# First norm of a hybrid encoder block on one Trainium2 core: gain multiplied as rows land, reciprocal root applied by a diagonal product, six idle products

## The chip, the cores and the metric

The kernel runs on one core of a Trainium2 chip (trn2). A core has TensorE (PE, with its weight loads PEld), VectorE (DVE), ScalarE (ACT), GpSimd (POOL) and SyncE (SP, which only issues DMAs here), 128-partition memories SBUF and PSUM (8 banks of 512 f32 columns), and 16 DMA engines. The metric is the device time of one execution in microseconds (us).

## The reference, cut to what matters

The block works on x with 512 rows (frames) of 1024 values. The change lies in the first norm and what feeds the first projection:

```python
def rms_norm(x, g):
    xf = x.astype(jnp.float32)
    y = xf * lax.rsqrt(jnp.mean(xf * xf, axis=-1, keepdims=True) + EPS)
    return (y * g.astype(jnp.float32)).astype(x.dtype)
...
def mixer(h, w_in, ...):
    proj = h @ w_in                       # 1024 x 4136
...
    for l in range(DEPTH):                # DEPTH = 1
        h = rms_norm(x, g_mix[l])
        x = x + mixer(h, w_in[l], ...)    # conv branch, indexer with top-k, sparse attention, gates, w_out
        h = rms_norm(x, g_ffn[l])
        x = x + hier_moe(h, ...)          # routed experts, 2 of 32 for each row
    return rms_norm(x, g_final)
```

## The kernel before, in words

The program is written out by hand for each engine, with semaphores between them: `pe.wait_ge(S["h_ready"], b + 1)` makes TensorE wait until the semaphore h_ready has counted to b + 1. An engine runs its instructions in the order in which they are written, so that order is the order of the work. Nothing is scheduled by a planner.

The 512 rows lie in four blocks of 128 (b = 0 to 3, TB = 4). SyncE issues their four loads first (ld_x), ScalarE issues the load of g_mix (ld_gmix), then SyncE the small part of w_in and the first two tiles of w_in, 256 columns each.

First norm, for each block of rows:

- ScalarE squares the 1024 columns and sums them into ss (L1163), semaphore ss_done.
- VectorE makes mean square plus EPS of it (`mean_square`, L1419), semaphore var_ready.
- GpSimd raises it to the power -0.5 (L539), semaphore rstd_ready. This is the "root" of a block, rs[:, 0, b].
- VectorE scales the block with root and gain in one instruction (L1438), semaphore h_ready. The result, hrow, lies in the tile that the trace calls region.
- TensorE transposes it in eight 128x128 pieces into two PSUM banks (L693), four pieces to a bank; xt_mm counts banks, n = 2b + kh. Banks 4 to 7 are used in turn, so bank n + 4 waits for h_lo of n (hlo_ready).
- ScalarE rounds a bank to fp32r (h_hi, L1172, hhi_ready), and VectorE takes the rest, bank minus h_hi (h_lo, L1430, `h_low`, hlo_ready).

When all eight h_lo are there, TensorE starts on the projection: units 0 to 32, each with 8 steps of k, and 3 products in each step (L708: hi x hi, hi x lo, lo x hi). The weights are split in the same way: ScalarE makes part 0 (L1117, w_hi), GpSimd part 1 (L561, w_lo). Unit u + 2 is split once unit u's last product is done (unit_mm). Unit 0 has 40 columns of weights, the others 128. ScalarE's splits of units 0 and 1 stand between its h_hi 3 and h_hi 4.

Behind the projection come indexer and top-k, attention, the convolution branch, the output product, the second norm with the router, and a loop over tiles of expert rows for which SyncE streams the experts' weights.

bm is a tile of 4 x 512 columns. Its part 0 is set to zero by GpSimd at the start, its part 2 is free until the top-k. ones_b is a 128x128 bf16 tile of ones, ident the f32 identity; both are ready with consts_ready 1.

Of the kernel before, what the change touches and what calls it, by code (L numbers as in the profile page):

```python
# [19 lines left out]
BF16 = mybir.dt.bfloat16  # L20
# [3 lines left out]
ALU = mybir.AluOpType  # L24
# [3 lines left out]
P = 128  # L28
BANK = 512
# [37 lines left out]
def build(nc, x, g_mix, w_in, conv_w, conv_b, conv_ln_g, conv_ln_b, w_conv_out, w_attn_out, w_out,  # L67
          rel_bias, g_ffn, w_gr, b_gr, w_er, b_er, w_e_gate, w_e_up, w_e_down, g_final, out):
    _, T, D = x.shape
    TB = T // P  # L70
    KD = D // P
# [28 lines left out]
    with ExitStack() as ctx:  # L100
# [25 lines left out]
        hrow = r1[:, 0:4096].rearrange("p (b n) -> p b n", b=TB)  # L126
# [44 lines left out]
        score, work = bm[:, 2, :], bm[:, 3, :]  # L171
        ring = bm
# [120 lines left out]
        names = """consts_ready ss_done var_ready rstd_ready h_ready cv_mm cv_ev xt_mm hhi_ready hlo_ready  # L293
# [385 lines left out]
        def _(pe):  # L679
# [3 lines left out]
            def transpose_rows(rows, ready, mm_sem, ev_sem, banks, after=None):  # L683

                for b in range(TB):
                    pe.wait_ge(ready, b + 1)
                    view = rows[:, b, :].rearrange("p (q k) -> p k q", k=KD)
                    for kh in range(2):
                        n = 2 * b + kh
                        if n >= len(banks):  # L690
                            pe.wait_ge(ev_sem, n - len(banks) + 1)
                        for kk in range(4):
                            last = tr(bank[banks[n % len(banks)]][:, kk * P:(kk + 1) * P], view[:, 4 * kh + kk, :],  # L693
                                      ident[:])
                        last.then_inc(mm_sem, 1)
                    if after and b:
                        after(b - 1)
                if after:
                    after(TB - 1)

            transpose_rows(hrow, S["h_ready"], S["xt_mm"], S["hlo_ready"], (4, 5, 6, 7))
# [704 lines left out]
        def _(dve):  # L1406
# [25 lines left out]

            mean_square(0, 0)
            for b in range(TB):
                if b + 1 < TB:
                    mean_square(0, b + 1)
                dve.wait_ge(S["rstd_ready"], b + 1)
                v.scalar_tensor_tensor(hrow[:, b, :], xr[:, b, :], rs[:, 0, b:b + 1], gmix, ALU.mult, ALU.mult)\  # L1438
                    .then_inc(S["h_ready"], 1)
                if b >= 2:  # L1440
                    h_low(2 * b - 4)
                    h_low(2 * b - 3)
            for n in range(2 * TB - 4, 2 * TB):
                h_low(n)
# [444 lines left out]
```

## Time and profile before

| | |
|---|---|
| time, median of 3 runs | 660.34 us (658.94 to 660.87) |
| the profiled execution's own time | 660.56 us |
| its span, from the first instruction to the last | 658.5 us |
| mean granted clock of TensorE | 0.96 |
| TensorE busy | 585.3 us (89% of the span) |
| VectorE busy | 344.7 us (52%) |
| ScalarE busy | 256.3 us (39%) |
| GpSimd busy | 294.9 us (45%) |

The span is that of the profiled execution, and its own time stands 2 us above it. Busy shares are means over a program whose stages have different limits; what a change in the first 20 us is worth is to be read there. The granted clock is a share of TensorE's full 2.4 GHz.

### The profile page before, as it was taken

Reading aid. Unit: us, or ns where it says so; the run is one execution under the profiler, and the core shown is the slowest. Engines: PE = TensorE matmul, PEld = TensorE weight load, DVE = VectorE, ACT = ScalarE, POOL = GpSimd, SP = SyncE. Lnnn points to the kernel's source line nnn. Section 1 sums busy time; section 2 is a strip of 40 time slices with the busy share of each in tenths; the row PEclk is TensorE's granted clock in tenths of the full one; section 3 lists DMA queues with packets and bytes.
Section 4 is the critical chain, followed back from the end, with each engine's and each line's share of the span. In section 5 each row is a group of like instructions: output and inputs, shape, how many; then the busy total and the mean of one; then the engine's idle time right before and its main releaser. Section 6 shows DMA issues by size and latency. Waiting matters only on the chain.

```text
span 658.5 us, 12493 instructions
## 1 busy us (share of the span) xinstructions
PE 585.3 (89%) x4383; PEld 381.0 (58%) x4388; DVE 344.7 (52%) x855; ACT 256.3 (39%) x444; POOL 294.9 (45%) x466
## 2 busy tenths in 40 slices
PE   3899999999999999999999976985898899888973
PEld 3577788877666676877888632432344444444431
DVE  4428999999979996269222683110112111211156
ACT  6345333244755675454313103331243233334212
POOL 5344344469996321445550016453255445444421
PEclk9899999999999999899999697997899999999977
DMA  9032732622222024032259999999998999999853
GB/s 297 23 111 65 226 94 67 137 64 65 64 65 65 0 75 181 1 128 73 87 191 356 378 397 352 408 407 408 409 401 325 410 410 407 409 400 398 342 230 127
DMA packets 64609, 149.09 MB, mean 226 GB/s; under 512 B 14372, under 2 KB 30756, under 8 KB 64574
## 3 DMA queue, kind: packets, MB, share of 16 engines
q1 hardware_dynamic: 59150, 139.90, 57.4%
q0 software_dynamic: 5280, 8.22, 3.4%
q10 hardware_dynamic: 144, 0.52, 0.3%
q8 instruction: 20, 0.33, 0.2%
q14 instruction: 15, 0.12, 0.0%
HBM read 145.11 MB, written 12.60 MB: 240 GB/s over the span
## 4 chain that ended last, share of the span: by engine, by line
PE 56%; DVE 20%; DMA 9%; SPq 6%; issue 4%; ACT 3%; POOL 1%; DVEq 0%; POOLq 0%; ACTq 0%
PE bank L708 28%; PE bank L1026 9%; PE bank L1043 6%; DVE bm L1481 5%; SPq L433 4%; DVE m L1480 4%; DMA region<-in_w_e_down 3%; DMA conv_buf<-in_w_e_down 3%; DVE conv_buf L1472 3%; PE bank L786 2%; PE bank L989 2%; DMA region<-expert_rows 2%; PE bank L819 2%; SPq L443 2%; PE bank L936 1%
## 5 line engine op out<-in xcount | busy, mean ns | idle before, releaser
L708 PE MATMUL bank<-h_hi,w_part 128*128 128x512 f32 (+1 forms) x528 | 174.3, 400 | 1.7 <-DVE h_lo L1430 1.7
L561 POOL TENSOR_TENSOR w_part<-region,w_part 128x1024 fp32r<-128x1024 f32 (+1 forms) x52 | 109.8, 2112 | 146.5 <-ACT w_part L1117 146.5
L708 PEld LDWEIGHTS bank<-h_hi,w_part 128*128 128x128 f32 (+1 forms) x528 | 98.3, 186 | 29.1 <-issue 6.1
L708 PE MATMUL bank<-h_lo,w_part 128*128 128x512 f32 (+1 forms) x264 | 103.5, 392 | 0.0
L1807 DVE TENSOR_TENSOR mask_b<-mask_b,bank 128x128 f32<-128x128 f32 x30 | 8.6, 287 | 176.0 <-ACT mask_b L1380 101.4
L1026 PE MATMUL bank<-region,kT 128*32 128x256 f32 x1408 | 83.9, 391 | 8.8 <-DMA region<-in_w_e_up 5.8
L1117 ACT ACTIVATE w_part<-region 128x1024 fp32r<-128x1024 f32 (+1 forms) x52 | 48.0, 925 | 106.1 <-PE bank L708 105.9
L611 POOL TENSOR_TENSOR carrier<-mhalf 128x1 f32<-128x1 f32 x183 | 32.8, 197 | 114.8 <-ACT qT L1387 97.5
L1515 DVE SCALAR_TENSOR_TENSOR bank<-glu,cv,bank 128x256 f32<-128x256 f32 x196 | 78.6, 476 | 0.0
L1026 PEld LDWEIGHTS bank<-region,kT 128*32 128x32 f32 x1408 | 47.4, 113 | 51.5 <-issue 19.3
L1043 PE MATMUL bank<-region,mask_b 128*32 128x512 f32 x352 | 44.5, 624 | 12.0 <-DVE mask_b L1810 8.9
L708 PEld LDWEIGHTS bank<-h_lo,w_part 128*128 128x128 f32 (+1 forms) x264 | 49.3, 187 | 9.9 <-issue 0.5
L1387 ACT ACTIVATE qT<-bank 128x512 f32 x28 | 16.7, 597 | 84.7 <-PE bank L1043 84.7
L626 POOL DMA_INDIRECT bm<-h_rows,gi x34 | 36.5, 1073 | 5.0 <-issue 0.2
L669 POOL DMA_INDIRECT expert_rows<-qT,si x30 | 30.7, 1023 | 13.5 <-issue 13.3
L1380 ACT ACT_TABLE_LOAD x28 | 35.9, 1283 | 0.5
L1380 ACT ACTIVATE mask_b<-bank 128x128 f32<-128x128 f32 x30 | 8.3, 277 | 62.0 <-PE bank L1026 60.3
L1026 PE MATMUL bank<-gates,kT 128*32 128x256 f32 x512 | 29.4, 380 | 2.2 <-DMA gates<-in_w_e_up 1.2
L989 PE MATMUL bank<-ident,v_rows 128*128 128x128 f32 x124 | 23.5, 313 | 6.5 <-DVE v_rows L1802 5.7
L989 PEld LDWEIGHTS bank<-ident,v_rows 128*128 128x128 f32 x124 | 17.4, 209 | 20.0 <-issue 13.9
L1043 PEld LDWEIGHTS bank<-region,mask_b 128*32 128x32 f32 x352 | 9.8, 112 | 29.8 <-issue 28.4
L1026 PEld LDWEIGHTS bank<-gates,kT 128*32 128x32 f32 x512 | 16.9, 110 | 17.6 <-issue 7.3
(289 smaller groups left out, 926.2 us busy)
## 6 DMA issues: line engine op xcount, KB each, us to landing
region<-in_w_e_down SPq DMA_DIRECT2D x22, 1024.0 KB
region<-in_w_e_gate SPq DMA_DIRECT2D x44, 512.0 KB
region<-in_w_e_up SPq DMA_DIRECT2D x44, 512.0 KB
region<-in_w_in SPq DMA_DIRECT2D x16, 1024.0 KB, 6.1
conv_buf<-in_w_e_down SPq DMA_DIRECT2D x10, 1024.0 KB
gates<-in_w_e_gate SPq DMA_DIRECT2D x20, 512.0 KB
gates<-in_w_e_up SPq DMA_DIRECT2D x20, 512.0 KB
region<-in_w_out SPq DMA_DIRECT2D x2, 2048.0 KB, 8.1
```

The lines of the kernel that those rows point to most:

```text
L561: g.tensor_tensor(unit_part(u, 1), unit_raw(u), unit_part(u, 0).bitcast(F32), ALU.subtract)\
L611: ins = g.tensor_tensor(carrier[:, n:n + 1], mhalf[:], mhalf[:], ALU.add)
L626: g.indirect_dma_start(out=ring[:, u, :], out_offset=None, in_=h2_halves, in_offset=bass.IndirectOffsetOnAxis(ap=gi1[:, u:u + 1], axis=0), ...
L669: g.indirect_dma_start(out=y_halves, out_offset=bass.IndirectOffsetOnAxis(ap=si1[:, q:q + 1], axis=0), in_=ys[:, q, :], in_offset=None, bo ...
L708: last = mm(out_, a_parts[p], b_parts[q], start=start and x_ == 0, stop=stop and x_ == 2)
L989: last = tr(bank[6 + k // 2][:, k % 2 * P:(k % 2 + 1) * P], view[:, k, :], ident[:])
L1026: last = mm(bank[0][32 * c:32 * c + 32, 0:FF], xTs[:, k, at_:at_ + 32], w_gu[slot][:, e, :, half, k, j * P:(j + 1) * P], start=(half == 0 ...
L1043: last = mm(bank[2][32 * c:32 * c + 32, :], hidT[:, at_:at_ + 32], w_dn[slot][:, e, j, n * BANK:(n + 1) * BANK], start=(j == 0), stop=(j = ...
L1117: a(unit_part(u, 0), unit_raw(u), ACT.Copy).then_inc(S["w_hi"], 1)
L1380: a(sil, bank[0][:, 0:P], ACT.Silu).then_inc(S["silu_g"], 1)
L1481: link(v.match_replace(work[:, 0:n], m8[:], src[:, 0:n], NEG))
L1515: ins = v.scalar_tensor_tensor(out_, shifted, cv[:, c, j:j + 1], so_far, ALU.mult, ALU.add)
```

## The change

The gain is multiplied into a block as soon as it has landed, without the root (`gain_rows`). VectorE then makes a 128x128 diagonal with the block's roots (`rstd_diag`, into bm's part 2), and TensorE, in place of transposing with the identity, multiplies the block's pieces with that diagonal, which transposes and scales in one. Behind the products of blocks 1, 2 and 3 stand one, one and four bf16 products of 512 columns (ones_b by the zeros in bm) whose result in bank 2 nobody reads. The helper `transpose_rows`, whose `after` nobody used, is gone.

```diff
@@ -169,6 +169,7 @@
         score, work = bm[:, 2, :], bm[:, 3, :]
+        rdiag = bm[:, 2, :].rearrange("p (b n) -> p b n", b=TB)
...
@@ -680,25 +681,21 @@
             pe.wait_ge(S["consts_ready"], 1)
-            def transpose_rows(rows, ready, mm_sem, ev_sem, banks, after=None):
-
-                for b in range(TB):
-                    pe.wait_ge(ready, b + 1)
-                    view = rows[:, b, :].rearrange("p (q k) -> p k q", k=KD)
-                    for kh in range(2):
-                        n = 2 * b + kh
-                        if n >= len(banks):
-                            pe.wait_ge(ev_sem, n - len(banks) + 1)
-                        for kk in range(4):
-                            last = tr(bank[banks[n % len(banks)]][:, kk * P:(kk + 1) * P], view[:, 4 * kh + kk, :],
-                                      ident[:])
-                        last.then_inc(mm_sem, 1)
...
-            transpose_rows(hrow, S["h_ready"], S["xt_mm"], S["hlo_ready"], (4, 5, 6, 7))
+            idle_rows = bm[:, 0, :].bitcast(BF16)[:, 0:BANK]
+            for b in range(TB):
+                pe.wait_ge(S["h_ready"], b + 1)
+                pe.wait_ge(S["rdiag_ready"], b + 1)
+                view = hrow[:, b, :].rearrange("p (q k) -> p k q", k=KD)
+                for kh in range(2):
+                    n = 2 * b + kh
+                    if n >= 4:
+                        pe.wait_ge(S["hlo_ready"], n - 3)
+                    for kk in range(4):
+                        last = mm(bank[4 + n % 4][:, kk * P:(kk + 1) * P], view[:, 4 * kh + kk, :], rdiag[:, b, :],
+                                  start=True, stop=True)
+                    last.then_inc(S["xt_mm"], 1)
+                for _ in range((0, 1, 1, 4)[b]):
+                    mm(bank[2][:], ones_b[:], idle_rows, start=True, stop=True)
             pe.wait_ge(S["hlo_ready"], 2 * TB)
...
@@ -1430,17 +1427,33 @@
+            def gain_rows(b):
+
+                dve.wait_ge(ld_x[b], 16)
+                v.tensor_tensor(hrow[:, b, :], xr[:, b, :], gmix, ALU.mult).then_inc(S["h_ready"], 1)
+
+            def rstd_diag(b):
+
+                dve.wait_ge(S["consts_ready"], 1)
+                dve.wait_ge(S["rstd_ready"], b + 1)
+                v.tensor_scalar(rdiag[:, b, :], ident[:], rs[:, 0, b:b + 1], None, ALU.mult)\
+                    .then_inc(S["rdiag_ready"], 1)
+
+            gain_rows(0)
             mean_square(0, 0)
-            for b in range(TB):
-                if b + 1 < TB:
-                    mean_square(0, b + 1)
-                dve.wait_ge(S["rstd_ready"], b + 1)
-                v.scalar_tensor_tensor(hrow[:, b, :], xr[:, b, :], rs[:, 0, b:b + 1], gmix, ALU.mult, ALU.mult)\
-                    .then_inc(S["h_ready"], 1)
-                if b >= 2:
-                    h_low(2 * b - 4)
-                    h_low(2 * b - 3)
-            for n in range(2 * TB - 4, 2 * TB):
+            gain_rows(1)
+            rstd_diag(0)
+            mean_square(0, 1)
+            gain_rows(2)
+            rstd_diag(1)
+            mean_square(0, 2)
+            gain_rows(3)
+            rstd_diag(2)
+            mean_square(0, 3)
+            h_low(0)
+            h_low(1)
+            rstd_diag(3)
+            for n in range(2, 2 * TB):
                 h_low(n)
```

VectorE's queue from its first instruction on, before. The names in brackets are the semaphores waited for; ss is the mean square, region the scaled rows:

```order
L1419 TENSOR_SCALAR ss<-ss 128x1 [waits ss_done,ld_gmix]
L1419 TENSOR_SCALAR ss<-ss 128x1 [waits ss_done]
L1438 SCALAR_TENSOR_TENSOR region<-x_rows,rs,gates 128x1024 [waits rstd_ready]
L1419 TENSOR_SCALAR ss<-ss 128x1 [waits ss_done]
L1438 SCALAR_TENSOR_TENSOR region<-x_rows,rs,gates 128x1024 [waits rstd_ready]
L1419 TENSOR_SCALAR ss<-ss 128x1 [waits ss_done]
L1438 SCALAR_TENSOR_TENSOR region<-x_rows,rs,gates 128x1024 [waits rstd_ready]
L1430 TENSOR_TENSOR h_lo<-bank,h_hi 128x4x128 [waits hhi_ready] x2
L1438 SCALAR_TENSOR_TENSOR region<-x_rows,rs,gates 128x1024 [waits rstd_ready]
L1430 TENSOR_TENSOR h_lo<-bank,h_hi 128x4x128 [waits hhi_ready] x6
```

The same place in the change, from the second block's multiply on (ahead of it stand the first block's multiply, which waits for ld_x0 and ld_gmix, and its mean square; bm<-ident,rs is the diagonal):

```order
L1433 TENSOR_TENSOR region<-x_rows,gates 128x1024 [waits ld_x1]
L1439 TENSOR_SCALAR bm<-ident,rs 128x128 [waits rstd_ready,consts_ready]
L1416 TENSOR_SCALAR ss<-ss 128x1 [waits ss_done]
L1433 TENSOR_TENSOR region<-x_rows,gates 128x1024 [waits ld_x2]
L1439 TENSOR_SCALAR bm<-ident,rs 128x128 [waits rstd_ready,consts_ready]
L1416 TENSOR_SCALAR ss<-ss 128x1 [waits ss_done]
L1433 TENSOR_TENSOR region<-x_rows,gates 128x1024 [waits ld_x3]
L1439 TENSOR_SCALAR bm<-ident,rs 128x128 [waits rstd_ready,consts_ready]
L1416 TENSOR_SCALAR ss<-ss 128x1 [waits ss_done]
L1427 TENSOR_TENSOR h_lo<-bank,h_hi 128x4x128 [waits hhi_ready] x2
L1439 TENSOR_SCALAR bm<-ident,rs 128x128 [waits rstd_ready,consts_ready]
L1427 TENSOR_TENSOR h_lo<-bank,h_hi 128x4x128 [waits hhi_ready] x6
```

The 1024-column operations no longer wait for the root and all stand ahead of the first h_lo; the wait for the root has moved to four 128-column operations, the first three of which stand ahead of the next mean square.

TensorE's queue from the third block of rows to the first projection products, before:

```order
L693 MATMUL bank<-ident,region 128x128 [waits hlo_ready,h_ready]
L693 MATMUL bank<-ident,region 128x128 x3
L693 MATMUL bank<-ident,region 128x128 [waits hlo_ready]
L693 MATMUL bank<-ident,region 128x128 x3
L708 MATMUL bank<-h_hi,w_part 40x512 [waits w_lo,hlo_ready]
L708 MATMUL bank<-h_lo,w_part 40x512
```

The same place in the change, from the product behind the second block on (bm<- is the diagonal in L694, the zeros in L698):

```order
L698 MATMUL bank<-bm,ones_b 128x512
L694 MATMUL bank<-bm,region 128x128 [waits hlo_ready,rdiag_ready,h_ready]
L694 MATMUL bank<-bm,region 128x128 x3
L694 MATMUL bank<-bm,region 128x128 [waits hlo_ready]
L694 MATMUL bank<-bm,region 128x128 x3
L698 MATMUL bank<-bm,ones_b 128x512 x4
L705 MATMUL bank<-h_hi,w_part 40x512 [waits w_lo,hlo_ready]
L705 MATMUL bank<-h_lo,w_part 40x512
```

The products stand where the transposes stood, with one more semaphore to wait for, and the four idle products fill the place between the last block and the projection.

## Rows read from the trace of the kernel before

**Rows 1.** The page's part 4, the chain that ended last, by line.
```profile
PE bank L708 28%; PE bank L1026 9%; PE bank L1043 6%; DVE bm L1481 5%; SPq L433 4%; DVE m L1480 4%; DMA region<-in_w_e_down 3%; DMA conv_buf<-in_w_e_down 3%; DVE conv_buf L1472 3%; PE bank L786 2%; PE bank L989 2%; DMA region<-expert_rows 2%; PE bank L819 2%; SPq L443 2%; PE bank L936 1%
```

**Rows 2.** Chain of waits, 0 to 60 us: start us, us, what.
```profile
18.45 0.69 DVE h_lo L1430
...
19.19 23.54 PE bank L708 x96
```

**Rows 3.** Time line, GpSimd, then VectorE: start us, us, instruction [idle before <-releaser].
```profile
7.75 0.56 POOL L539 TENSOR_TENSOR rs<-ss,mhalf 128x1 f32<-128x1 f32 x1 [3.89 <-DVE ss L1419]
...
9.05 1.52 POOL L539 TENSOR_TENSOR rs<-ss,mhalf 128x1 f32<-128x1 f32 x1 [0.74 <-DVE ss L1419]
...
10.55 0.54 POOL L539 TENSOR_TENSOR rs<-ss,mhalf 128x1 f32<-128x1 f32 x1
...
12.04 1.52 POOL L539 TENSOR_TENSOR rs<-ss,mhalf 128x1 f32<-128x1 f32 x1 [0.95 <-DVE ss L1419]
...
8.89 1.28 DVE L1438 SCALAR_TENSOR_TENSOR region<-x_rows,rs,gates 128x1024 f32<-128x1024 f32 x1
...
10.61 1.28 DVE L1438 SCALAR_TENSOR_TENSOR region<-x_rows,rs,gates 128x1024 f32<-128x1024 f32 x1 [0.35 <-POOL rs L539]
...
11.87 1.27 DVE L1438 SCALAR_TENSOR_TENSOR region<-x_rows,rs,gates 128x1024 f32<-128x1024 f32 x1
...
15.46 3.67 DVE L1430 TENSOR_TENSOR h_lo<-bank,h_hi 128x512 fp32r<-128x512 f32 x6
```

**Rows 4.** Stretches: length, PE, PEld, DVE, ACT, POOL busy (xcount), granted clock, DMA, GB/s.
```profile
17.50:18.98 1.48, 0.01 (x1) 0.00 (x0) 1.48 (x3) 0.64 (x2) 1.48 (x1) 1.00 0.06 25
18.99:22.39 3.40, 3.20 (x8) 1.49 (x9) 2.50 (x32) 0.00 (x0) 0.22 (x1) 0.50 0.01 1
22.40:25.80 3.40, 3.40 (x16) 1.63 (x15) 0.04 (x1) 0.00 (x0) 0.00 (x0) 1.00 0.00 0
```

**Rows 5.** Time line, ScalarE, squares, first h_hi, first large split.
```profile
6.18 1.06 ACT L1163 ACTIVATE gates<-x_rows 128x1024 f32<-128x1024 f32 x1 [3.65 <-DMA x_rows<-in_x]
...
7.63 1.06 ACT L1163 ACTIVATE gates<-x_rows 128x1024 f32<-128x1024 f32 x1 [0.31 <-DMA x_rows<-in_x]
...
11.51 0.60 ACT L1172 ACTIVATE h_hi<-bank 128x512 fp32r<-128x512 f32 x1
...
14.85 1.05 ACT L1117 ACTIVATE w_part<-region 128x1024 fp32r<-128x1024 f32 x1
```

**Rows 6.** DMA issues, 0 to 40 us: KB, us from issue to landing.
```profile
gates<-in_g_mix ACTq DMA_DIRECT2D x1, 512.0 KB, 5.5
```

**Rows 7.** Line L1602, an existing diagonal: ns min/median/max, first and last start.
```profile
L1602 DVE TENSOR_SCALAR bm<-ident,rs x4: 278/279/289, 269.3 to 269.9; 128x128 f32<-128x128 f32 x4
```

**Rows 8.** Time line, TensorE: transposes; plain f32 products; bf16 products.
```profile
10.31 5.46 PE L693 MATMUL bank<-ident,region 128*128 128x128 f32 x24 [10.31 <-DVE region L1438]
...
16.29 1.22 PE L693 MATMUL bank<-ident,region 128*128 128x128 f32 x8 [0.52 <-DVE h_lo L1430]
...
255.29 3.67 PE L848 MATMUL bank<-conv_buf,ones 128*128 128x512 f32 x8 [1.29 <-issue]
...
367.22 1.90 PE L936 MATMUL bank<-wr,bm 128*128 128x36 f32 x8
...
384.77 3.19 PE L965 MATMUL bank<-mask_b,ones_b 128*128 128x512 bf16 x14
```

**Rows 9.** Time line, GpSimd, part 1 of unit 2's weights.
```profile
27.64 2.39 POOL L561 TENSOR_TENSOR w_part<-region,w_part 128x1024 fp32r<-128x1024 f32 x1 [8.44 <-ACT w_part L1117]
```

**Rows 10.** Stretches, columns as in rows 4; the clock falls behind the last three.
```profile
388.00:394.00 6.00, 4.18 (x96) 2.76 (x96) 3.97 (x23) 0.00 (x0) 2.54 (x6) 1.00 1.01 375
394.00:397.80 3.80, 0.00 (x0) 0.00 (x0) 3.57 (x8) 0.00 (x0) 0.92 (x3) 1.00 1.01 373
449.00:452.40 3.40, 1.28 (x12) 0.42 (x16) 0.00 (x0) 0.00 (x0) 0.00 (x0) 1.00 1.04 405
626.00:629.90 3.90, 1.67 (x13) 0.85 (x17) 0.93 (x3) 0.66 (x2) 1.82 (x6) 1.00 1.03 413
```

More of the change, by code:

```diff
@@ L291, in build @@
         zeroed = sem("zeroed")
-        names = """consts_ready ss_done var_ready rstd_ready h_ready cv_mm cv_ev xt_mm hhi_ready hlo_ready
+        names = """consts_ready rdiag_ready ss_done var_ready rstd_ready h_ready cv_mm cv_ev xt_mm hhi_ready hlo_ready
             g_ready w_hi w_lo unit_mm unit_ev index_lo glu_done conv_step vt_mm vt_ev ix_mm ix_relu ix_acc
@@ L682, in _ @@
             pe.wait_ge(S["consts_ready"], 1)
-            def transpose_rows(rows, ready, mm_sem, ev_sem, banks, after=None):
-                for b in range(TB):
-                    pe.wait_ge(ready, b + 1)
-                    view = rows[:, b, :].rearrange("p (q k) -> p k q", k=KD)
-                    for kh in range(2):
-                        n = 2 * b + kh
-                        if n >= len(banks):
-                            pe.wait_ge(ev_sem, n - len(banks) + 1)
-                        for kk in range(4):
-                            last = tr(bank[banks[n % len(banks)]][:, kk * P:(kk + 1) * P], view[:, 4 * kh + kk, :],
-                                      ident[:])
-                        last.then_inc(mm_sem, 1)
[L696 to L699, printed above, removed]
-            transpose_rows(hrow, S["h_ready"], S["xt_mm"], S["hlo_ready"], (4, 5, 6, 7))
+            idle_rows = bm[:, 0, :].bitcast(BF16)[:, 0:BANK]
[13 more added lines that the diff above has]
+                    mm(bank[2][:], ones_b[:], idle_rows, start=True, stop=True)
             pe.wait_ge(S["hlo_ready"], 2 * TB)
```

## The prediction, on record before the changed kernel was run

> **What bounds the kernel now.** I read the page's chain first: the projection products of L708 hold 28% of it, more than any other line, and the two VectorE lines of the top-k 9% [rows 1]. So time at the front is worth something only if it moves the first L708 product, or makes these products faster. Next comes the chain of waits over the first 60 us [rows 2]: VectorE's last h_lo ends at 19.14, and at 19.19 TensorE starts 96 products that take 23.54 us without a pause. What holds VectorE up to there is on the time line [rows 3]: from 8.89 to 19.14 it works through four row scalings (L1438) and eight h_lo, with one idle gap of 0.35 us.
>
> The third view is TensorE's clock [rows 4]. From 17.50 to 18.98 TensorE ran nothing, and from 18.99 to 22.39 the granted clock is 0.50, the lower level (1.2 GHz), after which it is 1.00 again. 8 products lie in the slow stretch, 16 in the one from 22.40 to 25.80. Of the slow stretch TensorE works 3.2 us (from 19.19), and half of that is lost: **1.6 us**. As a check, the remaining 88 of the 96 products take 23.54 - 3.3 = 20.2 us, 0.23 each, against 3.3 / 8 = 0.42 for the first eight; 8 x 0.19 is 1.5. So two losses lie here: a VectorE queue that ends at 19.14, and a cold start.
>
> **The change part by part.**
> *The gain multiply.* It takes the place of L1438, reads x and g alone and waits for two landings and no root. ScalarE's first square starts at 6.18, when x0 has landed [rows 5]; g_mix is issued at 0.8 and lands 5.5 us later, at 6.3 [rows 6]. Row 0 can start at 6.4 instead of 8.89. No row has a multiply of two SBUF operands of 1024 columns. Bounds: six h_lo of 512 columns take 3.67, 0.60 each, so twice the columns take at least 1.2; the old scaling of 1024 takes 1.28 alone, 1.2 in a queue [rows 3]. I take the old one's. Four of them cost what the four old ones did: the multiply is moved, not shortened.
>
> *The diagonals.* Four operations ident x column, a form that L1602 has: 0.28 us [rows 7], some 0.2 in a queue. They add 0.8 us to VectorE ahead of the last h_lo, and four new waits for a root. Behind each wait stand the next mean square and the next gain multiply.
>
> *The root on GpSimd, and what stands in its way.* Here the change gives back most of its head start. Roots 0 and 2 take 0.56 and 0.54 us, roots 1 and 3 take 1.52 [rows 3]. The short ones began before an L1438, the long ones inside one, and these end 0.4 us behind it (8.89 + 1.28 = 10.17, root 10.57; 11.87 + 1.27 = 13.14, root 13.56). So a root asked for during such an operation waits for its end. In the new order the mean squares 0 to 2 are each followed at once by a gain multiply, and then by the diagonal that needs the root: three roots of four are held, where two were.
> The Trainium skill (SBUF — State Buffer, "Who interferes with whom") says that a VectorE instruction with two SBUF inputs contends with a GpSimd instruction that reads SBUF, and whichever comes second is blocked. The trace agrees: 1.52 against 0.56 us.
>
> The queue by hand, in us: gain 0 from 6.4 to 7.7; mean square 0 at 7.6; gain 1 7.7 to 9.0 (x1 is there at 7.63 [rows 5]); root 0, asked for at 7.9, is held to 9.4; diagonal 0 to 9.75; mean square 1 at 9.65; gain 2 9.7 to 11.0; root 1 at 11.4; diagonal 1 to 11.8; mean square 2 at 11.7; gain 3 11.75 to 13.05; root 2 at 13.45; diagonal 2 to 13.8; mean square 3 at 13.7; h_lo 0 and 1 from 13.8 to 15.0 (root 3 runs beside them in 0.56, since they read PSUM and one SBUF tile); diagonal 3 at 15.0; six h_lo from 15.2: 15.2 + 6 x 0.60 = 18.8, the last one's own end 18.9. TensorE starts at 19.0 instead of 19.19: **0.2 us**.
>
> Is VectorE still last? TensorE's row 0 starts at 9.9 instead of 10.31. Row 2 then waits for h_lo 0 (14.5), row 3 for h_lo 2 (15.9), and ends at 17.2. ScalarE's last two h_hi at 0.60 each end at about 18.1, the last h_lo starts at 18.2. There is 0.1 us of room.
>
> *Products in place of transposes.* 32 plain f32 products of 128 columns. The trace has plain f32 as 8 of 512 columns in 3.67 at full clock (0.43 start to start, 0.11 for 128 columns), and as 8 of 36 columns with fresh 128x128 weights in 1.90 at half clock (0.21 each). The transposes took 5.46 for 24 and 1.22 for 8, which is 0.23 and 0.15 with the gaps in them [rows 8]. Bounds: 0.11 at full clock if weight load and product overlap, and twice that if one follows the other. L708 overlaps them (512 columns in 0.23), so I take 0.11, and 0.21 at half clock: no change.
> The Trainium skill (Perfetto Trace Analysis, "Transposes") wants transposes as transposes and not as standard matmuls, and TensorE: Matmul & The Clock Gate ("Terms") gives the transpose mode a factor of 4 for FP32. With that factor the 32 products would add 3 x 32 x 0.11 = 11 us. No row of plain f32 bears the factor out.
>
> *Six idle products.* 512 columns bf16: 14 in 3.19, 0.22 us each at full clock [rows 8], twice that at half. The one behind row 1 lies in the wait for h_lo 0 (14.0 to 14.6). The one behind row 2 ends near 16.1, when row 3 may start: 0 to 0.1. The four behind row 3 run from 17.2 to 18.1, ahead of the last h_lo at 18.9, so they are free; at half clock they would take 1.7.
>
> *The clock.* This is the large term. Before, TensorE had 8 short products from 16.29 on and idled from 17.5. Now it works from 16.1 to 18.1 and idles 0.9 us. Does that hold the clock at 1.00? Later falls come behind 3.8 us without a product, behind 1.28 us busy in 3.40, and behind 1.67 in 3.90; 4.18 busy in 6.00 kept 1.00 [rows 10]. Here TensorE is busy for about 2.3 us between 15.6 and 19.0, which stands with the stretch that kept it. So the first 8 products run at 0.23 each: **1.6 us**.
>
> *What passes it on.* Each later split on ScalarE waits for unit_mm, GpSimd for ScalarE, and the loads of w_in for GpSimd. GpSimd stands idle 8.44 us until 27.64 [rows 9], so a first unit of 5.6 us in place of 7.3 still covers it; unit 1's second part is there by 20 and needed at 24.6. All behind 19.2 starts 1.8 us earlier, and later loads are issued on semaphores of the same program and move along.
>
> **The sum.** 0.2 + 1.6 = 1.8 us. The profiled execution took 660.56, so 658.8. The median of the runs, 660.34, lies 0.2 under it: **658.6 us**. A measurement of this kernel tells about 0.3% from no change, 2.0 us: the forecast lies just inside.
>
> **The rivals.**
> 1. *The clock falls all the same*, or it had not fallen in most runs before (they span 658.94 to 660.87, about one such loss). For it: what decides a fall is read from few cases. Against: some 2.3 us busy is far from 1.3. Then 0.2 us is left: 660.1. Chance 0.2.
> 2. *The gain multiply doesn't hold the roots*, its form being new. VectorE is then through its gains at 12.3, and ScalarE becomes the end: its 1024-column split (1.05, starting at 14.85 now, I estimate 14.2 at the earliest), four h_hi at 0.55 to 0.60 and one h_lo give 18.3 [rows 5]. 0.8 + 1.6 us: 657.9. Two equally long roots speak against it. Chance 0.12.
> 3. *A plain f32 product of 128 columns takes twice a transpose*, load and product one behind the other; this is the one on the other side. Row 0 then holds TensorE 3.4 us at half clock (9.9 to 13.3), row 1 until 16.5, rows 2 and 3 1.8 us each at full clock, to 20.5. With h_hi and h_lo behind, the start is at 21.8, 2.6 later, less 1.6: 661.3. With the clock at half through rows 2 and 3 it is 3.4 more, 664.7. It decides from some 0.12 us a product upward, as there is 0.1 us of room. The skill's rule on transposes stands beside it. Chance 0.08, half of it beyond +0.3%.
>
> **How the numbers follow.** The forecast has 0.6, with its own range of 657.6 to 659.8, since the later falls of the clock [rows 10] meet a shifted program and give or take a us. The range that holds 8 in 10 is 657.2 to 660.3: rival 2 and a lucky forecast lie at its lower end, rival 1 at its upper, rival 3 and half of rival 1 beyond. Faster by over 0.3% (under 658.3): 0.26 of the forecast's 0.6, as it lies close to the line, and 0.10 of rival 2: 0.36. Slower: 0.04 of rival 3 and 0.02 of rival 1. Within: 0.58.
>
> **What would show it.** Gain multiplies of 1.2 to 1.3 us from 6.4 on; roots 0 to 2 at about 1.5 us and root 3 at 0.56; VectorE idle some 0.5 us ahead of the first three diagonals; products of the new L694 at 0.21 us in rows 0 and 1 and 0.11 in row 3; the first L705 near 19.0, 0.23 us between products, and a granted clock of 1.00 from 19 to 22.4. The prediction is wrong if the clock reads 0.50 there, if the first L705 comes after 19.2, or if the 96 products' end (42.73 before) has not moved by 1.8 us.

## The result and the profile after

The changed kernel is slower. Its median is **667.26 us** (664.24 to 668.37, 4 runs), against 659.64 us (658.56 to 660.87, 4 runs) of the kernel before on the same chip: a ratio of **1.0102**, 95% interval 1.0082 to 1.0122, or 6.7 us; the two medians themselves lie 7.6 us apart. The prediction was 658.6 us, with a range that ended at 660.3. It was wrong, and in the direction that it had given 0.06.

The profiled execution of the changed kernel took 664.24 us (span 662.3, mean granted clock 0.968). It is the fastest of the four, so its end lies some 3 us ahead of the median's; its front is what the study needs.

The chain that ended last has a line that was not among its first 15 before [rows 1]: L694, the 32 products that took the transposes' place. The page's part 4 of the changed kernel, by engine and by line:

```profile
PE 58%; DVE 19%; DMA 9%; SPq 5%; issue 4%; ACT 3%; POOL 1%; DVEq 0%; POOLq 0%; ACTq 0%
PE bank L705 27%; PE bank L1023 10%; PE bank L1040 6%; DVE bm L1494 5%; DVE m L1493 4%; SPq L434 3%; DMA conv_buf<-in_w_e_down 3%; DMA region<-in_w_e_up 3%; DVE conv_buf L1485 3%; PE bank L694 2%; PE bank L783 2%; DMA region<-expert_rows 2%
```

The chain of waits over the first 60 us of the changed kernel, to be held against [rows 2]:

```profile
0.80 5.74 DMA gates<-in_g_mix
...
6.57 1.23 DVE region L1433
...
8.01 1.48 POOL rs L540
...
9.58 0.30 DVE bm L1439
9.88 0.14 issue
10.02 7.88 PE bank L694 x32
17.90 0.21 PE bank L698
18.11 3.71 PE bank L694 x16
21.82 0.05 issue
21.88 3.89 PE bank L694 x16
25.77 0.02 issue
25.79 0.61 ACT h_hi L1169
...
26.42 0.70 DVE h_lo L1427
...
27.17 22.07 PE bank L705 x96
```

Before, VectorE held TensorE up until 19.19. Now TensorE holds itself up: from 10.02 to 25.77 it does nothing but the products of L694 and two idle ones, then come one h_hi and one h_lo, and the first projection product (L705, the old L708) starts at **27.17, 8.0 us later**. The 96 products then take 22.07 us instead of 23.54, as the clock stays up, so that they end at 49.24, 6.5 us later than before (19.19 + 23.54 = 42.73). Everything up to 346 us keeps this distance. Further on, this one execution gains back 0.9 us by 374 us and 1.9 more by its end, where its clock falls at other places than in the trace before.

The count tells how 32 products can take so long. The line's own record in the changed kernel (ns min/median/max, first and last start), with its weight loads:

```profile
L694 PEld LDWEIGHTS bank<-bm,region x64: 312/336/340, 10.0 to 25.2; 128*128 128x128 f32 x64
L694 PE MATMUL bank<-bm,region x64: 292/403/574, 10.0 to 25.4; 128*128 128x128 f32 x64
```

The program writes 4 x 8 = 32 products; the trace has **64** of them, each with a weight load of its own. A plain f32 product is two passes. That was there to be read before: in the program `channel_mean` is four products, and the trace shows eight under L848.

```python
for c in range(CC):                       # CC = 4
    last = mm(bank[6][:], ones[:], yv[:, c, :], start=(c == 0), stop=(c == CC - 1))
```

It stands as x8 in [rows 8], and I took the eight for eight products. L936 is 32 products in the program as well (4 blocks, 8 steps of k) and has 64 records in the trace.

The second half is that each pass takes 0.24 us, where the transposes took 0.21 at half and 0.11 at full clock. It takes that at full clock too, which the clock had reached by then: an idle product of 512 columns takes 0.38 us at 17.73, against 0.63 at half clock (e1 at 13.80). Two stretches of the changed kernel (columns as in [rows 4]), the first inside the products of L694, the second the first 3.4 us of the projection:

```profile
16.40:20.00 3.60, 3.60 (x18) 3.59 (x17) 1.38 (x2) 2.27 (x5) 1.23 (x4) 1.00 0.07 21
...
27.20:30.60 3.40, 3.40 (x15) 1.72 (x16) 2.22 (x30) 0.00 (x0) 0.00 (x0) 1.00 0.03 7
```

In the first stretch the weight loads are busy for 3.59 of 3.60 us, beside 1.72 of 3.40 in the second, at the same granted clock. So per product it is 2 x 0.24 = 0.48 us, where 0.21 and 0.11 had been put into the sum.

### The profile page after: what moved, and what is told of

It reads as the page before. It is cut to its first block, busy times and chain, and to the rows that moved or that the text cites. A ratio compares the mean times of both kernels' runs of the same rounds, so it can differ in the third digit from the quotient of the medians.

```text
span 662.3 us, 12577 instructions
## 1 busy us (share of the span) xinstructions
PE 591.1 (89%) x4420; PEld 388.7 (59%) x4426; DVE 346.0 (52%) x859; ACT 256.7 (39%) x444; POOL 294.8 (45%) x466
## 4 chain that ended last, share of the span: by engine, by line
PE 58%; DVE 19%; DMA 9%; SPq 5%; issue 4%; ACT 3%; POOL 1%; DVEq 0%; POOLq 0%; ACTq 0%
PE bank L705 27%; PE bank L1023 10%; PE bank L1040 6%; DVE bm L1494 5%; DVE m L1493 4%; SPq L434 3%; DMA conv_buf<-in_w_e_down 3%; DMA region<-in_w_e_up 3%; DVE conv_buf L1485 3%; PE bank L694 2%; PE bank L783 2%; DMA region<-expert_rows 2%; PE bank L986 2%; PE bank L816 2%; PE bank L804 1%
## 5 line engine op out<-in xcount | busy, mean ns | idle before, releaser
L705 PE MATMUL bank<-h_hi,w_part 128*128 128x512 f32 (+1 forms) x528 | 173.1, 397 | 0.6 <-DVE h_lo L1427 0.6
L705 PEld LDWEIGHTS bank<-h_hi,w_part 128*128 128x128 f32 (+1 forms) x528 | 97.9, 186 | 27.6 <-issue 4.9
L705 PE MATMUL bank<-h_lo,w_part 128*128 128x512 f32 (+1 forms) x264 | 102.9, 390 | 0.0
L705 PEld LDWEIGHTS bank<-h_lo,w_part 128*128 128x128 f32 (+1 forms) x264 | 49.1, 186 | 9.7
L670 POOL DMA_INDIRECT expert_rows<-qT,si x30 | 30.8, 1025 | 13.1 <-issue 12.8
L570 POOL TENSOR_SCALAR bm<-glu,cv 128x512 f32<-128x512 f32 x17 | 26.7, 1570 | 0.9
```

The lines of the kernel that those rows point to most:

```text
L670: g.indirect_dma_start(out=y_halves, out_offset=bass.IndirectOffsetOnAxis(ap=si1[:, q:q + 1], axis=0), in_=ys[:, q, :], in_offset=None, bo ...
L705: last = mm(out_, a_parts[p], b_parts[q], start=start and x_ == 0, stop=stop and x_ == 2)
```

## The experiments

The markers are the start of the first projection product, and the end of the 96 (their starts say when the first norm is done; the changed kernel has 27.17 and 49.24, the trace before 19.19 and 42.73). Medians are followed by lowest and highest, ratios are against the kernel before on the same chip, with 95% intervals.

### e1: transposes in place of the products

Everything of the change but the swap: VectorE's order, the diagonals and the idle products stay.

```diff
-  last = mm(bank[4 + n % 4][:, kk * P:(kk + 1) * P], view[:, 4 * kh + kk, :], rdiag[:, b, :],
-            start=True, stop=True)
+  last = tr(bank[4 + n % 4][:, kk * P:(kk + 1) * P], view[:, 4 * kh + kk, :], ident[:])
```

> The changed kernel with identity transposes in place of the diagonal products; the root is computed and waited for but left out of h, so routing and the expert stage may differ and the first 340 us are what is read. Theory A (all of the loss is the plain f32 products, which run as two passes each): h_lo 7 ends near 18.9, the first projection product starts at 19.0 and the clock holds, so stages behind 20 us stand 1.8 us earlier than before (chain of waits: end of the 96 products at 41.0 against 42.73), total 658. Rival B (the held roots or the new VectorE order lose time too): first projection product after 19.5, total 660 or more.

Measured: 657.29 us (656.3 to 660.8, 10 runs), ratio 0.9983 (0.9964 to 1.0002). TensorE's time line in this kernel:

```profile
10.06 3.94 PE L694 MATMUL bank<-ident,region 128*128 128x128 f32 x16 [10.06 <-DVE bm L1438]
...
14.71 1.22 PE L694 MATMUL bank<-ident,region 128*128 128x128 f32 x8 [0.28 <-DVE h_lo L1426]
...
16.10 1.22 PE L694 MATMUL bank<-ident,region 128*128 128x128 f32 x8
17.16 1.03 PE L697 MATMUL bank<-bm,ones_b 128*128 128x512 bf16 x4
19.00 0.43 PE L704 MATMUL bank<-h_hi,w_part 128*40 128x512 f32 x1 [0.81 <-DVE h_lo L1426]
```

The transposes are 16 + 8 + 8 = 32 records for 32 operations, 8 of them in 1.22 us. The first projection product starts at 19.00, which is the number that the sum in the prediction had come to, and the 96 end at 41.07. The total is worth less than the front here: the root is missing from h, so the expert stage may have had other rows to work on. So all the rest of the change does at the front what was forecast of it, and the whole loss comes with the swap.

### e8: the swap alone

The other way round: the kernel before, with the 32 transposes written as products with the identity, and nothing else changed.

```diff
-  last = tr(bank[banks[n % len(banks)]][:, kk * P:(kk + 1) * P], view[:, 4 * kh + kk, :],
-            ident[:])
+  last = mm(bank[banks[n % len(banks)]][:, kk * P:(kk + 1) * P], view[:, 4 * kh + kk, :],
+            ident[:], start=True, stop=True)
```

> The kernel before with plain f32 products by the identity in place of its 32 transposes, and nothing else changed. Theory (the products alone make the loss): 64 passes of 0.24 us from 10.3 on, first projection product near 27, total 6 to 8 us over before, within 1 us of the changed kernel. Rival (a part of the loss is the new VectorE order): first projection product before 25, total under 5 us over before.

Measured: 668.39 us (666.7 to 669.08, 4 runs), ratio 1.0136 (1.0102 to 1.0169). Its chain of waits at the front:

```profile
10.31 15.60 PE bank L693 x64
...
27.31 22.07 PE bank L708 x96
```

64 passes in 15.60 us are 0.244 each. The clock stayed at 1.00 over the pause of 1.4 us behind them, with no idle product in it (the 96 take 22.07). This one edit to the kernel before puts the first projection product at 27.31 and makes the whole slowdown. With e1 the place of the loss is settled; what remains is why it is 0.48 us for a product.

### e2: adjacent columns

The pieces of h are taken in steps of 8 words (`(q k)`), so that a piece's 128 columns lie 8 words apart. Here each piece is 128 adjacent columns, and the rows of w_in are loaded in the order that belongs to it; the result is the same.

```diff
-  view = hrow[:, b, :].rearrange("p (q k) -> p k q", k=KD)
+  view = hrow[:, b, :].rearrange("p (k q) -> p k q", k=KD)
...
-  w_in2 = w_in[0].rearrange("(p k) n -> p k n", k=KD)
+  w_in2 = w_in[0].rearrange("(k p) n -> p k n", k=KD)
```

> The changed kernel with pieces of 128 adjacent columns as weights in place of every 8th column, and w_in's rows loaded in the order that fits (k p in place of p k); nothing is left out. Theory A1 (a pass is held to 0.24 us by the step of 8 words in the weights): passes of 0.21 us in rows 0 and 1 and 0.11 in rows 2 and 3, row 3 done near 20.8, first projection product near 22, total 1 to 2 us over before (661 to 662). Rival A2 (a pass is held by weight load and product following one another, whatever the step): still 0.24 a pass, first projection product at 27.2, total 666 to 667.

Measured: 659.02 us (658.17 to 662.87), ratio 1.0015 (0.9994 to 1.0037). The chain of waits, and the record of L694:

```profile
9.86 6.15 PE bank L694 x32
...
16.23 1.78 PE bank L694 x16
18.06 1.96 PE bank L694 x16
...
21.42 22.07 PE bank L705 x96
```

```profile
L694 PEld LDWEIGHTS bank<-bm,region x64: 190/192/334, 9.8 to 19.6; 128*128 128x128 f32 x64
L694 PE MATMUL bank<-bm,region x64: 273/275/551, 9.9 to 19.7; 128*128 128x128 f32 x64
```

There are still 64 passes, but 16 of them take 1.78 us, 0.11 each, at full clock (0.213 at half). The weight load's median falls from 336 to 192 ns. So the two causes come apart: the count of two passes stands by itself, and the step of 8 words is what holds each pass at 0.24. With adjacent columns the first projection product starts at 21.42, 5.75 us earlier than in the changed kernel and still 2.4 later than in e1. That rest is the second pass. (g_mix lands at slightly different times; the first product starts at 9.86 in e2, 10.02 in the changed kernel and 10.06 in e1, so both differences are good to 0.2 us.)

### e9 and e6: steps of 2 and of 4 words

The rows of h are numbered in another way here, which no longer fits w_in, so the projection's values are not the reference's; shapes and work at the front are. The totals are of other data and say little.

```diff
-  view = hrow[:, b, :].rearrange("p (q k) -> p k q", k=KD)
+  view = hrow[:, b, :].rearrange("p (c q k) -> p c k q", c=4, k=2)   # e9; e6: c=2, k=4
```

> The changed kernel with weights of every 2nd column in place of every 8th, so that h is permuted against w_in and only the first 50 us are read. Steps of 4 and 8 gave 0.23 and 0.24 us a pass, adjacent columns 0.11. Theory (any step holds a pass up alike): 0.23 again. Rival (two words that lie side by side in 8 bytes still come together, or the cost grows with the step): 0.11 to 0.2.

> The changed kernel with weights of every 4th column in place of every 8th, so that h is permuted against w_in and only the first 50 us are read. Theory (the cost grows with the distance between the words that a partition hands over): less than 0.24 us for a pass at full clock, more than 0.11. Rival (any step is as bad, or a step under 8 is as good as none): 0.24, or 0.11.

Measured: 658.18 us for e9 and 667.85 for e6 (one run each). TensorE's time line, row 3 of e9, and of e6 the chain's piece for the same row:

```profile
18.14 2.04 PE L694 MATMUL bank<-bm,region 128*128 128x128 f32 x16
...
21.59 0.43 PE L705 MATMUL bank<-h_hi,w_part 128*40 128x512 f32 x1 [0.55 <-DVE h_lo L1427]
```

```profile
21.52 3.80 PE bank L694 x16
...
26.73 22.08 PE bank L705 x96
```

A pass takes 0.118 us at a step of 2 (1.89 us for 16 in its chain) and 0.233 to 0.238 at a step of 4, against 0.111 at 1 and 0.24 at 8. The cost is not proportional to the step: it lies between 2 and 4 words and is all there at 4.

### e5: the step on the moving operand

I had come to think that it is the weight load alone which suffers from the step, since it is what is busy for 3.59 of 3.60 us. Here the two operands change places, so that the diagonal is the weight and the stepped tile is streamed. The piece of h comes out untransposed, so h is another matrix.

```diff
-  last = mm(bank[4 + n % 4][:, kk * P:(kk + 1) * P], view[:, 4 * kh + kk, :], rdiag[:, b, :], ...)
+  last = mm(bank[4 + n % 4][:, kk * P:(kk + 1) * P], rdiag[:, b, :], view[:, 4 * kh + kk, :], ...)
```

> The changed kernel with the roles in its products swapped: the diagonal is the weights, the piece with the step of 8 words streams through. The result is the scaled block untransposed, so h is another matrix and only the first 50 us are read. Theory (it is the weight load that the step holds up): passes of 0.21 us at half clock and 0.11 at full, two for each product, first projection product near 21.4 as with adjacent columns. Rival (any plain f32 pass that touches a tile with a step takes 0.24): first projection product near 27.

Measured: 674.01 us (one run; as h is another matrix, what follows it works on other data, and the total says little). The chain's piece for row 3, and the record of the weight loads:

```profile
21.71 3.90 PE bank L694 x16
...
27.01 22.08 PE bank L705 x96
```

```profile
L694 PEld LDWEIGHTS bank<-region,bm x64: 188/209/338, 9.8 to 25.0; 128*128 128x128 f32 x64
```

The weight loads are short now (median 209 ns in place of 336), and a pass still takes 0.23 to 0.24 us. The theory of the weight load falls: reading an f32 tile in a step of 4 words or more holds a pass at 0.23 to 0.24, whichever of the two operands it is.

### e7: one pass, with fp32r

fp32r is the type in which the projection's parts h_hi and h_lo already lie. Here VectorE writes the gain's result and the diagonals in it (rounded to that type), and the product reads them; the step stays at 8.

```diff
-  v.tensor_tensor(hrow[:, b, :], xr[:, b, :], gmix, ALU.mult)
+  v.tensor_tensor(hrow_r[:, b, :], xr[:, b, :], gmix, ALU.mult)
...
-  last = mm(..., view[:, 4 * kh + kk, :], rdiag[:, b, :], ...)
+  last = mm(..., view[:, 4 * kh + kk, :], rdiag_r[:, b, :], ...)     # view of hrow_r
```

> The changed kernel with the multiplied rows and the diagonals rounded to fp32r, the format of the projection's parts, in place of f32; the step of 8 stays. Theory (a plain f32 product is two passes with a weight load each, an fp32r one is a single pass): 32 records in place of 64, row 3 done by about 19, first projection product at 19.0 to 20. Rival (two passes stay, or a single pass takes as long as the two): first projection product after 22.

Measured: 660.58 us (one run). The record of the products, in e7:

```profile
L697 PE MATMUL bank<-rdiag_r,hrow_r x32: 416/442/667, 10.0 to 18.6; 128*128 128x128 f32 x32
```

32 records for 32 products: one pass each, so the doubling belongs to the plain f32 type. From one start to the next they stand 0.24 us apart, as every pass with a step of 8. The first projection product starts at 20.42. It is not at 19.0, as the clock stayed at half: the first ones of the 96 run at 0.42 until about 22.4, and the idle products take 0.43 to 0.45 each.

### e10 and e11: fp32r and adjacent columns, with and without the idle products

e10 is e7 with e2's two lines; e11 is e10 with `range((0, 0, 0, 0)[b])` for the idle products.

> The changed kernel with both mends: rows and diagonals rounded to fp32r, so one pass for each product, and weights of 128 adjacent columns with w_in's rows loaded in the order that fits; apart from the rounding nothing is left out. Theory (two passes and the step are the whole loss, and VectorE's queue and the clock behave as predicted): row 3's products done near 17, last h_lo ends at 18.9, first projection product at 19.0, clock 1.00 there, end of the 96 products at 41.0, total 1.5 to 2 us under before. Rival (a single pass with fresh weights of fp32r is slower than a transpose, as it was 0.24 us with the step): first projection product after 19.5, total as before.

> The kernel of the run before this one, without the six idle products. Theory (they keep the clock up over the wait for the last h_lo): first projection product at 19.0 all the same, granted clock 0.50 from about 19, end of the 96 products near 42.5, total 1 to 1.6 us over the run with them. Rival (products, in place of transposes, keep the clock up by themselves, as the page on TensorE suggests): clock 1.00, no difference.

Measured: e10 659.68 us (657.56 to 661.69, 12 runs), ratio 1.0010 (0.9992 to 1.0028); e11 660.00 us (658.93 to 662.09, 12 runs), ratio 1.0017 (1.0001 to 1.0033). TensorE's time line of e10, then the chain of e11:

```profile
14.64 1.94 PE L697 MATMUL bank<-rdiag_r,hrow_r 128*128 128x128 f32 x8 [0.26 <-DVE h_lo L1430]
...
16.47 2.16 PE L697 MATMUL bank<-rdiag_r,hrow_r 128*128 128x128 f32 x8
18.44 1.70 PE L701 MATMUL bank<-bm,ones_b 128*128 128x512 bf16 x4
20.05 0.43 PE L708 MATMUL bank<-h_hi,w_part 128*40 128x512 f32 x1
```

```profile
14.54 3.66 PE bank L697 x16
...
19.60 24.36 PE bank L708 x96
```

With both causes removed each product costs what a transpose costs at half clock, 0.21 us, but the gain that I had expected of e10 didn't come: the first projection product starts at 20.05 (e10) and 19.60 (e11), not at 19.0. Its eight products of row 3 take 2.16 us, where e1's eight transposes took 1.22: the clock was still at its lower level there, and came up at 19.8, against 14.6 in e1. In e11 it came up at 24.6, and the 96 products took 24.36 us in place of 22.07. (The column of the granted clock can't be used for this: it reads 1.00 ahead of a trace's first change of the clock. The distance of two products tells it, 0.42 us or 0.23.) So both lost at the front by a clock that came up later: the 96 end at 42.13 (e10) and 43.96 (e11), against 41.07 in e1. The totals barely show it.

At the lower clock the idle products weren't free either. The one behind row 2 pushed row 3 back: e10's last h_lo starts at 19.30 and e11's at 18.86, while row 2 had started only 0.1 us apart (14.64 and 14.54). By the prediction it was to cost 0 to 0.1 us.

Products as such don't keep the clock down. Here is an idle product from e2, whose other products are plain f32, and one from e10:

```profile
15.85 0.38 PE L698 MATMUL bank<-bm,ones_b 128*128 128x512 bf16 x1
```

```profile
16.38 0.65 PE L701 MATMUL bank<-bm,ones_b 128*128 128x512 bf16 x1
```

0.38 us is its time at full clock, 0.65 that at half. By the distances and lengths of TensorE's records in all 14 traces, the clock had come up between 13.1 and 16.4 us in the eleven whose front runs f32 transposes or plain f32 products, with and without the step. In the three with fp32r it came up at 22.4 (e7), 19.8 and 24.6.

### e3: the changed kernel without idle products

`range((0, 0, 0, 0)[b])` in the changed kernel.

> The changed kernel without its six idle products. Theory A (TensorE is busy with the products until 25.6, so the clock needs no help): first projection product 0 to 0.4 us earlier than in the changed kernel (26.8 to 27.2), clock 1.00 there, total 666 to 667. Rival: the clock falls behind the last product, 8 products at 0.42 us, total 1.6 us over the changed kernel.

Measured: 666.08 us (664.65 to 668.15, 4 runs), ratio 1.0108 (1.0077 to 1.0139). Three stretches of it, columns as in [rows 4]: the end of row 3's products, the pause behind them, the start of the projection.

```profile
24.00:25.20 1.20, 1.20 (x6) 1.17 (x5) 0.69 (x1) 0.09 (x1) 0.00 (x0) 1.00 0.00 0
25.20:26.70 1.50, 0.16 (x1) 0.00 (x0) 0.67 (x2) 0.60 (x1) 0.00 (x0) 1.00 0.00 0
26.80:30.20 3.40, 3.40 (x9) 1.46 (x10) 2.23 (x30) 0.00 (x0) 0.00 (x0) 0.51 0.03 7
```

The first projection product comes 0.4 us earlier than in the changed kernel (26.77), and the 96 end 1.2 us later (50.40), since the clock falls at 26.8, after 15.5 us in which TensorE was busy throughout by its records and 1.4 us in which it wasn't. With the four products in the pause (the changed kernel) it had not fallen; but neither had it in e8, which has the same products and a pause as long with nothing in it. I had expected 1.00 here. The totals tell the two apart by no more than their intervals.

### e4 and e12: the kernel before, with the idle products and as it is

e4 is the kernel before with the same 0, 1, 1 and 4 idle products behind its own transposes. e12 is the kernel before once more, for a second trace.

```diff
+  def idle(b):
+      for _ in range((0, 1, 1, 4)[b]):
+          mm(bank[2][:], ones_b[:], idle_rows, start=True, stop=True)
-  transpose_rows(hrow, S["h_ready"], S["xt_mm"], S["hlo_ready"], (4, 5, 6, 7))
+  transpose_rows(hrow, S["h_ready"], S["xt_mm"], S["hlo_ready"], (4, 5, 6, 7), idle)
```

> The kernel before with only the six idle products added, behind its transposes of blocks 1, 2 and 3. Theory (the clock term of the prediction stands by itself): first projection product at 19.2 as before, granted clock 1.00 from 19 to 22.4, end of the 96 products at 41.1 in place of 42.73, total 1.6 us under before. Rival: the clock falls all the same, total unchanged; or the idle products push row 3's transposes back by up to 0.4 us and the gain is 1.2.

> The kernel before once more, for its clock. Theory (the fall at 19 us is in most executions): granted clock 0.50 within 18 to 23 us, end of the 96 products 1.3 to 1.7 us later than at full clock (42.3 to 42.8). Rival (the first profile caught a rare one): 1.00 throughout and the end near 41.2, so that the idle products had nothing to win in most runs.

Measured: e4 658.38 us (656.93 to 660.77, 10 runs), ratio 0.9995 (0.9979 to 1.0010); e12 659.40 us (one run). The stretch in which the clock was at 0.50 in the first trace of before [rows 4], in e12 and then in e4:

```profile
18.99:22.39 3.40, 3.17 (x14) 1.64 (x15) 2.50 (x32) 0.00 (x0) 0.25 (x1) 1.00 0.01 1
```

```profile
18.99:22.39 3.40, 3.05 (x14) 1.53 (x15) 2.32 (x31) 0.00 (x0) 0.38 (x1) 1.00 0.01 3
```

Both read 1.00. In e4 the 96 products start at 19.34 and take 22.08, so the clock stayed up; but in e12 they start at 19.21 and take 22.08 too, with no idle product anywhere. The same kernel before has one trace with a fall of the clock at 19 us and one without. Taken over all runs: where the clock had come up before the pause, it fell behind it in two of the four traces without idle products (before and e3, not e12 and e8), and in none of the seven with them (the changed kernel, e1, e2, e4, e5, e6, e9). That points to idle products which work, but only in those executions in which the clock would have fallen, and 1.5 us each time. e4's total shows no gain beyond its interval, which reaches down to 1.4 us less.

## Why the prediction was wrong

**Steps that held.** g_mix lands at 6.54 (6.3 forecast), and the four gain multiplies take 1.22 to 1.23 us from 6.57 on (1.28, from 6.4 forecast). The roots are held as forecast; GpSimd's time line in the changed kernel, to be compared with [rows 3]:

```profile
8.01 1.47 POOL L540 TENSOR_TENSOR rs<-ss,mhalf 128x1 f32<-128x1 f32 x1 [4.15 <-DVE ss L1416]
10.01 1.47 POOL L540 TENSOR_TENSOR rs<-ss,mhalf 128x1 f32<-128x1 f32 x1 [0.53 <-DVE ss L1416]
12.01 1.46 POOL L540 TENSOR_TENSOR rs<-ss,mhalf 128x1 f32<-128x1 f32 x1 [0.53 <-DVE ss L1416]
14.01 0.55 POOL L540 TENSOR_TENSOR rs<-ss,mhalf 128x1 f32<-128x1 f32 x1 [0.54 <-DVE ss L1416]
```

Three roots of 1.5 us inside a gain multiply, the fourth of 0.55 without one. VectorE's diagonals take 0.29 us (0.28), with 0.52, 0.52 and 0.51 us idle ahead of the first three (some 0.5). Rival 2 is out. The products start at 10.02 (9.9). The queue by hand ended with an h_lo at 18.9 and TensorE at 19.0; where the transposes are kept (e1) it is 18.95 and 19.00. The last h_lo before, at 19.14, is now at 27.12 in the changed kernel for a reason that has nothing to do with VectorE: it idles 1.0 to 1.3 us ahead of each of the later h_lo.

**The step that failed** is "Products in place of transposes": "I take 0.11, and 0.21 at half clock: no change". The number was read off records and used for operations. "8 of 512 columns in 3.67 at full clock" are four products, 0.86 us of work for each and not 0.43, so for 128 columns 0.22 and not 0.11; "8 of 36 columns" are four as well. With the count right the rows of before give 0.42 us a product at half clock and 0.22 at full. That is the price which rival 3 was made with, and its start at 21.8 stands beside the 21.42 of e2. The step of 8 words in the weights was not considered at all: none of the plain f32 rows that the prediction read has one, and the transposes, which have it, don't pay for it (e1: 8 in 1.22 us). It is worth the other 5.75 us, by e2 against the changed kernel. The sum made with what was measured: 32 x 0.48 from 10.0 with two idle products of 0.2 between is 25.8, h_hi and h_lo put the start at 27.2, 8.0 us late, less the 1.5 us of clock that the first trace of before had lost: 660.56 + 6.5 = 667.1 us, beside a median of 667.26. That they meet to 0.2 us is luck, since executions of one kernel differ by 2 to 4 us: from the median before, 659.64, the same sum gives 666.1, and 667.6 if the clock had not fallen in most executions before.

**The rule that was set aside.** Behind this step the prediction named the Trainium skill (Perfetto Trace Analysis, "Transposes"; and TensorE: Matmul & The Clock Gate, "Terms", with its factor of 4 for FP32), estimated 11 us by it, and set it aside with "No row of plain f32 bears the factor out". The rows did bear out a part of it, to whoever counted. Measured at full clock the ratio of product to transpose is 2 with adjacent columns (0.22 to 0.11) and a little over 4 with the step of 8 (0.48 to 0.11); 8.2 us is what the swap cost at the first projection product, from e1's 19.00 to 27.17.

**The rivals.** Rival 3 had the right side, and its bound ("decides from some 0.12 us a product upward") was passed four times over. Its mechanism was not the one: load and pass overlap as before, and there are two of each. Its upper price, 664.7, was made with 0.42 us for a product; 0.48 at either clock and row 0 to row 3 alike gives what happened.

**The clock term** had the right mechanism for the trace that it was read from, and was put a little high: 1.6 us, where the 96 products take 22.07 in place of 23.54, 1.5 less. In e1 the clock was up from 14.6 on and the 96 products ended at 41.07, 1.66 us earlier than before, of a forecast 1.8. But the first part of rival 1, "it had not fallen in most runs before", has its case in e12, which shows the kernel before at full clock there. e1's ratio of 0.9983 (0.9964 to 1.0002) is 1.1 us, between the 0.2 and the 1.8 us of the sum, and within its interval both are possible; the missing root makes this total a weak witness besides. How often the clock of the kernel before falls at 19 us stays open; two traces don't tell it.

**"What would show it"** named the right places. The products of the new L694 were to be at 0.21 and 0.11, the first L705 near 19.0: these two are off. The clock did read 1.00 from 19 to 22.4, and from 27.2 to 30.6, as forecast.

No kernel here is clearly faster than the one before. e1 and e4 are nearest, with intervals that include 1, and e1 leaves the root out of h.

## What to carry to other kernels

Before a price is taken from a trace, count what the program issues at that line and hold it against the trace's count: a plain f32 product is two records, a transpose or an fp32r product is one. A transpose that becomes a product (to bring in a scale on the way) has to be paid for on TensorE, by a factor of two at least in f32 and by four where the tile is read in steps of 4 words or more; here a scaling that took VectorE hardly more time than the plain multiply does (1.28 us against 1.23) was given up for it. And a fall of the clock in one profile is a property of that execution until a second profile of the same kernel shows it.

## What the runs showed of the hardware

- **Two passes.** A plain f32 product has two TensorE records and two weight loads (64 for 32 in the changed kernel, e2, e5, e6, e8 and e9); a product of fp32r operands has one (32 for 32 in e7, e10, e11), and so has an f32 transpose (32 for 32 in e1 and before). A pass means one such record here, and it isn't as short as a bf16 product: in the trace of before one of 512 columns takes 0.43 us (L848) where a bf16 product takes 0.22 (L965) [rows 8], so that the whole f32 product takes four times a bf16 one.
- **The step.** A pass of 128x128 f32 at full clock takes 0.111 us with adjacent words, 0.118 with a step of 2, 0.233 to 0.24 with a step of 4 or 8; at a step of 8 it is 0.24 at half clock also (e7). It is much the same on either operand (0.233 in e5). An f32 transpose is not held: it takes 0.11 at full clock with a step of 8 (e1) and with adjacent columns (L928 in the trace of before). Why a transpose is spared, no run here tells.
- **When the clock comes up.** With f32 transposes or plain f32 products at the front it had reached 1.00 by 13.1 to 16.4 us in all eleven traces (14.6 in e1, 14.8 in e2). With one-pass fp32r products at 0.21 to 0.24 us, which by the records keep TensorE as busy as the transposes do, it came at 22.4 (e7), 19.8 (e10) and 24.6 (e11). So what an operation counts for there can't be read from busy time, and fp32r is the difference that goes with the delay; why was not tried. The Trainium skill (TensorE: Matmul & The Clock Gate, Part 4, "PE-mode transpose") says that the full clock doesn't engage for transposes in this mode. The trace of before doesn't agree: TensorE runs nothing but transposes up to 17.5 us, and the eight at 16.29 take 1.22 [rows 8], 0.11 each as at full clock, after 0.21 at first.
- **A fall behind full load.** In e3 the granted clock fell to its lower level at 26.8 us (0.51 over the stretch from there) although TensorE had been busy for all of the 15.5 us up to 25.4; only the 1.4 us behind lay idle. It stayed at 1.00 in the changed kernel, with four bf16 products in that place, and also in e8, with none.
